# Attention on TensorE: in a slot that has products with the values, the transpositions of the weights are issued ahead of those products

## The reference, cut to what matters

```python
def sb_block(q, k, v, bias, q_pos, k_pos):
    z = jnp.einsum('bqhd,bkhd->bhqk', q, k) * (SB_HEAD_DIM ** -0.5)
    z = z + bias[None, :, None, None]
    mask = k_pos[None, :] < q_pos[:, None]
    log_beta = jax.nn.log_sigmoid(z)
    log_keep = jnp.where(mask, jax.nn.log_sigmoid(-z), 0.0)
    later = lax.cumsum(log_keep, axis=3, reverse=True) - log_keep
    a = jnp.where(mask, jnp.exp(log_beta + later), 0.0)
    return jnp.einsum('bhqk,bkhd->bqhd', a, v)
```

## Time and profile before

| | |
|---|---|
| time, median of 3 runs | 1683.26 us (1683.05 to 1683.74) |
| profiled execution | 1683.39 us |
| its span, first to last instruction | 1681.6 us |
| TensorE busy | 1668.7 us, 99% |
| TensorE weight loads | 1463.4 us, 87% |
| VectorE busy | 1102.6 us, 66% |
| ScalarE busy | 794.6 us, 47% |
| GpSimd busy | 317.9 us, 19% |
| DMA | 170.66 MB, 101 GB/s |

### The profile page before, as it was taken

How to read it: one execution, slowest core, us unless ns; L and a number is a source line. 1 busy time by engine, 2 the same in 40 slices (tenths; PEclk the granted TensorE clock), 3 DMA queues, 4 the chain that set the end, 5 groups by cost and what they waited for, 6 DMA issues and landing times. The chain is left out here.

```text
span 1681.6 us, 27183 instructions
## 1 busy us (share of the span) xinstructions
PE 1668.7 (99%) x9107; PEld 1463.4 (87%) x9107; DVE 1102.6 (66%) x1608; ACT 794.6 (47%) x1389; POOL 317.9 (19%) x266
## 2 busy tenths in 40 slices
PE   9999999999999999999999999999999999999998
PEld 8999998999999989988888888888888788888886
DVE  7265246325533647547678888888888698776576
ACT  6445344444534453135444444444444444465675
POOL 1000000000000000003356666666664000000000
PEclk9999999999999999999999999999999999999999
DMA  5312221132123114443132222222222852345333
GB/s 177 102 55 74 78 78 56 57 99 68 61 66 94 51 62 149 155 164 121 62 97 79 79 78 76 73 73 79 79 79 90 300 192 78 94 146 188 108 125 119
DMA packets 176599, 170.66 MB, mean 101 GB/s; under 512 B 16207, under 2 KB 144555, under 8 KB 176492
## 3 DMA queue, kind: packets, MB, share of 16 engines
q1 hardware_dynamic: 165546, 164.41, 30.3%
q10 hardware_dynamic: 10946, 4.91, 1.0%
HBM read 129.66 MB, written 39.62 MB: 101 GB/s over the span
## 5 line engine op out<-in xcount | busy, mean ns | idle before, releaser
L2810 PE MATMUL pair<-xh,wh 128*128 128x384 f32 (+1 forms) x952 | 324.3, 341 | 0.0
L2812 PE MATMUL pair<-xh,wl 128*128 128x384 f32 (+1 forms) x952 | 311.2, 327 | 0.0
L2811 PE MATMUL pair<-xl,wh 128*128 128x384 f32 (+1 forms) x952 | 310.6, 326 | 0.0
L2810 PEld LDWEIGHTS pair<-xh,wh 128*128 128x128 f32 x952 | 179.2, 188 | 5.4 <-issue 4.0
L2811 PEld LDWEIGHTS pair<-xl,wh 128*128 128x128 f32 x952 | 179.3, 188 | 0.0
L2812 PEld LDWEIGHTS pair<-xh,wl 128*128 128x128 f32 x952 | 178.7, 188 | 0.0
L1073 POOL TENSOR_TENSOR srow<-hn,hn 128x512 f32<-128x512 f32 x8 | 12.0, 1506 | 804.1 <-DVE hn L2298 803.8
L3337 PE MATMUL pair<-woph,foph 128*128 128x512 f32 x308 | 120.7, 392 | 0.7 <-DVE fopl L2451 0.7
L3339 PE MATMUL pair<-woph,fopl 128*128 128x512 f32 x308 | 120.0, 390 | 0.0
L3338 PE MATMUL pair<-wopl,foph 128*128 128x512 f32 x308 | 119.9, 389 | 0.0
L1401 ACT ACTIVATE keep<-pair,bias 128x512 f32<-128x512 f32 (+4 forms) x100 | 58.2, 582 | 115.7 <-DVE pair L2151 71.5
(11 more groups left out here) (416 smaller groups left out, 4284.5 us busy)
## 6 DMA issues: line engine op xcount, KB each, us to landing
rawp<-in_w_up SPq DMA_DIRECT2D x88, 256.0 KB, 3.8
raw<-in_w_in SPq DMA_DIRECT2D x80, 256.0 KB, 3.2
wd<-in_w_down SPq DMA_DIRECT2D x55, 256.0 KB, 3.0
f_spill<-cv SPq DMA_DIRECT2D x22, 552.0 KB, 2.8
f<-f_spill SPq DMA_DIRECT2D x44, 256.0 KB, 5.5
gat<-gate_spill SPq DMA_DIRECT2D x16, 544.0 KB, 4.5
x_spill<-x SPq DMA_DIRECT2D x16, 512.0 KB, 3.0
gate_spill<-stg SPq DMA_DIRECT2D x32, 192.0 KB, 1.9
```

Of the source, the lines that this page charges most:

```text
L2810: t_.matmul(b, h, xhi, start=(k == 0), stop=False, skip_group_check=True)
L2811: t_.matmul(b, h, xlo, start=False, stop=False, skip_group_check=True)
L2812: ins = t_.matmul(b, l, xhi, start=False, stop=(k == KD - 1), skip_group_check=True)
```

## The change

The call of `weights_turned` moves from behind the call of `values` to ahead of it. Nothing is added or taken away.

```diff
                 for n in range(SLOTS):
                     if n % 2 and n < NSTEP and not opens(n - 2):
                         scores(n)
+                    if 0 <= n - 2 < NSTEP:
+                        weights_turned(n - 2)
                     if n in VALUES_AT:
                         values(VALUES_AT[n])
-                    if 0 <= n - 2 < NSTEP:
-                        weights_turned(n - 2)
                     for i in range(PIECES):
                         piece(*divmod(PIECES * n + i, KD))
```

## The result

The changed kernel takes 1686.43 us (median of 20 runs, 1686.25 to 1687.13) against 1683.59 us for the kernel before (20 runs): 2.84 us more, a ratio of 1.0016, 95% interval 1.0009 to 1.0023. Forecast were 1686.2 us and 2.95 us more, the former from the 1683.26 us of the first three runs. Two executions are left out of all that follows: one of the six of e5, which took 1837.42 us at a granted clock of 0.851, and one of the twelve of e7, which took 8415.35 us.

A forecast was written before the change was run, and what follows sets the result against it. TensorE's stream, busy 99% of the span, was taken as the bound. Slot 11's 2.60 us and slot 19's 0.35 us sum to 2.95, giving 1686.2 us on the median of 1683.26; range 1684.6 to 1687.4.

The forecast's parts named there:

- No gain to be had: Values' products in slots 11 and 19 wait for nothing today, so moving the transpositions gains zero.
- A new wait in slot 11: TensorE's transposition waits for VectorE's multiplication in four pairs: 0.60 or 0.70 us each, 2.60 us in all.
- Changes of form in slot 19: No wait, but dearer matmul form changes: 0.20 us in pair 1, 0.05 in each other pair, 0.35 in all.
- The unknown cost: Transposition to values of form 128*64, shown by no row: taken as 0.20 us; bounds over eight places -0.7 and +1.0.
- No wait: Rival: in slot 11 VectorE finishes in time, leaving 0.6 us more, 1683.9 us; chance 8%.
- Absorbed later: Rival: TensorE's later waits shrink, up to 2.9 us vanishes, 1683.3 us; chance 7%.
- dear change of form: Rival: transposition to values costs the upper bound, 3.9 us in all, 1687.2 us; chance 13%.
- Inside 0.2%: Whole kernel: 0.18% slower, just inside the 0.2% (3.37 us) a measurement can tell; chance of within 76%.
- shorter waits there: Small gain from shorter waits for weights in slot 10, given a third of a rival's 7%.

The follow-up runs named there:

- e5: Changed kernel with VectorE's subtraction (L1956) in slot 9 done twice: 1691.92 us over five executions, 8.2 over the kernel before, ratio 1.0048.
- e7: Kernel before with VectorE's subtraction (L1956) moved behind the multiplication of step 9: 1683.91 us over eleven executions, ratio 1.0003, no readable profile.
- e4: Changed kernel with VectorE's subtraction (L1956) moved behind the multiplication of step 9: 1684.23 us, 0.83 over the kernel before, ratio 1.0006.
- e3: Changed kernel with slot 11's transposition and values behind the third piece, slot 19 as in the kernel before: 1683.76 us, ratio 1.0002.
- e9: Changed kernel with slot 10's transpositions moved behind the slot's second piece: 1687.36 us, 3.6 over the kernel before, ratio 1.002.
- e2: Kernel before with transpositions first in slot 19 alone, slot 11 as before: 1684.03 us, 0.63 over the kernel before, ratio 1.0006.

## Why the prediction was right

- **No gain to be had.** Right. Nothing shrank by more than 0.1 us among TensorE's waits behind the start. The copy to wT was released by the transposition before and is released by the end of the values' products now. Against TensorE's second piece it came 0.1 us sooner (107.73 against 107.68 before, 108.25 against 108.30 after), as little as the prediction had said, and no wait of TensorE hung on it. Before and after, pair 1, slot 11:

```profile
107.73 0.28 ACT L1428 ACTIVATE wT<-pair 128x128 f32<-128x128 f32 x1 [1.40 <-PE pair L2764]
...
108.25 0.28 ACT L1428 ACTIVATE wT<-pair 128x128 f32<-128x128 f32 x1 [1.90 <-PE pair L2990]
```

- **A new wait in slot 11.** Right in place, cause and size. In pair 1 the multiplication ended 0.44 us after TensorE could have used it (105.43 against 104.84 + 0.15 = 104.99), the transposition followed 0.05 us later, and the four prices came out at 0.60, 0.71, 0.70 and 0.62 us for 0.60, 0.70, 0.70 and 0.60. e4 takes the wait away from VectorE's side, e3 from TensorE's, e5 enlarges it. The waits named for L2168 rose by 1.5 us, a little less than the 1.6 to 2.0 forecast, since that view counts only the idle time of the matmuls (0.33 us in pair 1, where the loads idled for 0.59). What made this step safe to forecast is that no row of VectorE's stream, from the subtraction at 103.34 to the multiplication, waits for TensorE. e9 shows the same: with TensorE 0.4 us earlier in pair 2, the multiplication came no sooner.
- **Changes of form in slot 19.** Right: 0.19 and three times 0.05 us. The profile shows it, the times alone would not: e2's interval includes no change.
- **The unknown cost.** The nearest row, 0.20 us to form 128*32, was the right one: e3 shows 0.20 to form 128*64. The bounds on both sides were not needed.
- **The rivals.** "No wait" was refuted by the profile after. "Absorbed later" too: the later waits stand as before, and e5's 5.1 us of added wait came out as 5.4 us of added time. The dear change of form was refuted by e3.
- **Inside 0.2%.** The measured 0.16% lies inside, and its interval reaches from 0.09% to 0.23%. That it was a slowdown is clear of the noise. That its size, 2.84 us, came within 0.1 us of the forecast is in part luck, since the interval is over 1 us to each side; the 2.96 us at the places against 2.95 is not.
- **A miss in the rivals.** For slot 10 I thought only of shorter waits there as a small gain of the change. That the wait of slot 10 was the lever, worth about 1 us in the kernel before, I did not see, though its row stood there.

## What to carry to other kernels

When a waiting instruction is moved ahead of work on the bound engine, compare two times in the trace: when its input ends, and when the engine would now reach it. If the work jumped over was covering the difference, the change costs that difference each time, unless a later wait absorbs it. In pair 1 it was 0.44 us of a price of 0.60; the rest is 0.05 until the load starts, and 0.06 and 0.05 for weight loads that stand exposed in the new order. A wait on the bound engine is removed by putting ready work ahead of it; check then whether the next wait hangs on the same slow engine, because if it does, the time is only moved.

## What was not expected of the hardware

The sequence of forms does not tell the whole price; the prediction had this from the rows of before, but the code alone would not have led one to expect it. The first instruction after a change of form starts together with its weight load (both at 108.04 for the piece in slot 11 after) instead of about 0.15 us behind it, and this costs more for a piece than for a transposition: from a piece's start to the next piece 0.25 us instead of 0.15, from a transposition to what follows 0.06 more than the usual 0.11. So two orders with the same number of changes of form differ by 0.05 us, seen alone in the slots 19 of pairs 2 to 4, and in all four slots 11 of e3 and of e4. The Trainium skill ("TensorEngine Tiling (Array Packing)", Key Properties) says that a change of the tiling mode drains TensorE; the trace agrees, with about 0.1 us for a change.

The time from the end of VectorE's multiplication to the start of the load that waits for it was 0.05 us in each of the seven such waits of the changed kernel, and it was no other in e5, where the loads had idled for up to 1.95 us.
